# Sixteen single gate groups, the key norm ahead of the decay sums, and new order tables in a two-block transformer kernel

## What is computed

```python
proj = h @ w_in                                   # q, k, v of 8 heads, gate z (2048), 16 logits
qkv = silu(causal_depthwise_conv(qkv, conv_w))    # 4 taps
q, k = l2_norm(q) * 128 ** -0.5, l2_norm(k)
beta, g = sigmoid(b_logit), -exp(a_log) * softplus(a_logit + dt_bias)
# chunked, per head: g = cumsum(g); decay = exp(g_i - g_j) on the lower triangle
lower = strict_tril(beta * (k @ k.T) * decay)
u, w = solve(I + lower, [v * beta, k * beta * exp(g)])
qk = (q @ k.T) * decay
for each chunk:
    v_new = u_i - w_i @ S
    o = (q * exp(g))_i @ S + qk_i @ v_new
    S = S * exp(g_last) + (k * exp(g_last - g))_i.T @ v_new
o = rms_norm(o, o_gain) * silu(z)
x = x + o @ w_out
```

## Time and profile before

| | |
|---|---|
| median of 3 runs | 1658.16 us (1657.97 to 1661.1) |
| the profiled execution's own time | 1661.27 us |
| its span from first to last instruction | 1659.5 us |
| mean granted TensorE clock | 0.981 |
| head loop | about 65 to 530 us |

### The profile page before, as it was taken

One profiled execution on the slowest core, in us unless ns is written; L12 is line 12 of the kernel. 1 busy time (PEld: TensorE's weight loads), 2 busy tenths in 40 slices (PEclk: granted clock), 3 DMA queues, 4 the chain that ended last, 5 costly groups with the idle time before them and its releaser, 6 DMA issues.

```text
span 1659.5 us, 20679 instructions
## 1 busy us (share of the span) xinstructions
PE 1578.6 (95%) x7686; PEld 1240.5 (75%) x7686; DVE 875.4 (53%) x1633; ACT 746.9 (45%) x1293; POOL 244.3 (15%) x451
## 2 busy tenths in 40 slices
PE   6789999998989999999999899999999999999998
PEld 5577888887777876777777687666577888888876
DVE  4666667666663554555555533544347334343466
ACT  4443454345444244566556523555455433232343
POOL 1033224332331100223222300000000000000000
PEclk9799999999999999999999899999999999999999
DMA  4121112111112323222222122111132323232221
GB/s 178 64 77 39 64 51 77 52 52 39 51 38 73 126 89 107 76 81 67 77 69 73 52 96 90 64 52 51 39 102 66 112 89 102 92 106 94 93 86 64
DMA packets 40163, 127.22 MB, mean 77 GB/s; under 512 B 4576, under 2 KB 9104, under 8 KB 40064
## 3 DMA queue, kind: packets, MB, share of 16 engines
q1 hardware_dynamic: 38112, 121.65, 22.6%
q0 software_dynamic: 1040, 3.27, 0.6%
q10 hardware_dynamic: 912, 0.99, 0.2%
HBM read 122.69 MB, written 2.15 MB: 75 GB/s over the span
## 4 chain that ended last, share of the span: by engine, by line
PE 81%; DVE 7%; ACT 7%; issue 3%; POOL 1%; DMA 1%; SPq 0%; ACTq 0%; DVEq 0%; POOLq 0%
PE ps L776 79%; ACT L L1655 3%; DVE wl L1848 2%; DVE L L2331 1%; PE ps L1108 1%; PE ps L901 1%; ACT wh L1255 1%; DVE qkv L1884 1%; DMA wraw<-in_wa 1%; DVE qb L1933 1%; POOL L L2614 1%; ACT L L1607 0%; DVE h L2460 0%; DVE U L2184 0%; ACT xm L1790 0%
## 5 line engine op out<-in xcount | busy, mean ns | idle before, releaser
L776 PE MATMUL ps<-xr,wh 128*128 128x512 f32 x2752 | 906.2, 411 | 16.7 <-DVE wl L1848 15.3
L776 PEld LDWEIGHTS ps<-xr,wh 128*128 128x128 f32 x2752 | 506.9, 191 | 146.4 <-issue 40.5
L776 PE MATMUL ps<-xr,wl 128*128 128x512 f32 x1376 | 544.9, 396 | 0.0
L1848 DVE TENSOR_TENSOR wl<-wraw,wh 128x1024 fp32r<-128x1024 f32 x214 | 262.6, 1233 | 171.4 <-ACT wh L1255 169.7
L776 PEld LDWEIGHTS ps<-xr,wl 128*128 128x128 f32 x1376 | 262.1, 190 | 57.9
L1255 ACT ACTIVATE wh<-wraw 128x1024 fp32r<-128x1024 f32 x214 | 222.3, 1049 | 89.2 <-PE ps L776 85.3
L776 PE MATMUL ps<-xm,wh 128*128 128x512 f32 x640 | 200.0, 394 | 6.7 <-DVE xm L2445 3.7
L776 PEld LDWEIGHTS ps<-xm,wh 128*128 128x128 f32 x640 | 120.3, 189 | 35.3 <-DVE xm L2445 5.0
L2614 POOL TENSOR_SCALAR L<-L,m 128x256 f32<-128x256 f32 (+1 forms) x128 | 80.5, 649 | 317.0 <-DVE m L2346 317.0
L776 PE MATMUL ps<-xm,wl 128*128 128x512 f32 x320 | 125.3, 392 | 0.0
L1884 DVE SCALAR_TENSOR_TENSOR qkv<-cin,gains,qkv 128x512 f32<-128x512 f32 x96 | 73.7, 769 | 4.0 <-ACT qkv L1283 2.9
(11 more groups left out here) (258 smaller groups left out, 1793.3 us busy)
## 6 DMA issues: line engine op xcount, KB each, us to landing
wraw<-in_wa SPq DMA_DIRECT2D x48, 512.0 KB, 3.7
wraw<-in_wb SPq DMA_DIRECT2D x32, 512.0 KB, 3.9
wraw<-in_wu SPq DMA_DIRECT2D x32, 512.0 KB, 3.6
wraw<-in_wd SPq DMA_DIRECT2D x32, 512.0 KB, 3.7
wraw<-in_wao SPq DMA_DIRECT2D x16, 512.0 KB, 3.7
wraw<-in_wbo SPq DMA_DIRECT2D x16, 512.0 KB, 3.8
wraw<-in_wc SPq DMA_DIRECT2D x16, 512.0 KB, 3.7
bias<-rel_rows SPq DMA_DIRECT2D x16, 256.0 KB, 4.2
```

Of the source, the lines that this page charges most:

```text
L776: return e.matmul(out, w, x, start=start, stop=stop, skip_group_check=True)
L1848: e.tensor_tensor(m.wl[:, i % N_SPLIT, :], m.raw[:, i % N_RAW, :], m.wh[:, i % N_SPLIT, :].bitcast(F), ALU.subtract).then_inc(s.wlo, 1)
```

## The change

Three things change together. The z products, until now 8 pairs of groups, are 16 single groups: six in pass 1, one in each of passes 2 to 5, two in pass 6, one in pass 7, three in pass 8. In `prep` the sum of squares of k (`ks`) and its norm stand ahead of the decay's sums (`G`) and its exponential, and DVE's `dv` moves from its first piece to its fourth, right ahead of `y`; POOL's mask moves with it. And every order table (`PLAN`) is new, with `STEADY` replaced by the entry "a". The number of instructions and their sizes stay the same.

```diff
 PRODUCTS = {
-    1: (("head", 0), ("head", 1), ("z", 0), ("z", 1)),
-    2: (("head", 2), ("z", 2)),
-    3: (("head", 3), ("z", 3)),
-    4: (("head", 4), ("z", 4)),
-    5: (("head", 5), ("z", 5)),
-    6: (("head", 6),),
-    7: (("head", 7),),
-    8: (("z", 6), ("z", 7)),
+    1: (("head", 0), ("head", 1)) + tuple(("z", n) for n in range(6)),
+    2: (("head", 2), ("z", 6)),
+    3: (("head", 3), ("z", 7)),
+    4: (("head", 4), ("z", 8)),
+    5: (("head", 5), ("z", 9)),
+    6: (("head", 6), ("z", 10), ("z", 11)),
+    7: (("head", 7), ("z", 12)),
+    8: (("z", 13), ("z", 14), ("z", 15)),
 }
 def groups_of(what, h):
-    return [[("wa", 6 * h + j)] for j in (range(4) if what == "head" else range(4, 6))]
+    if what == "z":
+        return [[("wa", 6 * (h // 2) + 4 + h % 2)]]
+    return [[("wa", 6 * h + j)] for j in range(4)]
 PLAN = {
-    0: plan("g5 g4 g6"),
-    1: plan("p0 p5 p4 p0 p2 p2 p3 p2 p2 p4 p3 p2 p1 p2"),
-    2: plan("q1 q0 p0 p4 q0 p0 q2 p1 q1 p0 q0 p3 q0 p1 q2 p2 r1 r0 p0 r1 p1 r1 p2 r0 p1 r3 p2 r3 r0 p1 r0 r2 r2"),
-    HEADS: plan("q1 p0 q0 p3 q3 p0 q2 p0 q2 p0 q2 p3 q2 p0 q1 p1 r3 r1 r2 p1 p3 p0 r2 r1 p2 r3 p2 r0 r4 p5 r1 r5 r3"),
-    HEADS + 1: plan("q2 q4 q2 q3 q3 q2 q2 q0 r3 r1 r2 r3 r4 r0 r1 r1 r7 r4 r3"),
+    "a0": plan("g10 g9 g17"),
+    "a1": plan("p5 p8 p2 p1 p2 p3 p10 p6 p6 p9 p6 p11 p14 p8"),
+    "a2": plan("p2 p0 p0 q1 p2 q3 q1 p0 q5 q2 q0 p0 q2 p0 q3 r0 p1 r3 r1 r0 r1 p0 r1 r1 r4 p0 p1 r0 r2 p2 p5 p0 r1"),
+    "a8": plan("p0 q1 p2 q3 q1 q0 p0 q0 p3 q0 p0 q0 p0 q0 p1 r1 r0 r1 r0 p0 r0 p2 p0 r0 p0 r0 p2 r5 p0 r1 p0 r2 r1"),
+    "a9": plan("q1 q5 q2 q5 q3 q1 q3 q2 r9 r1 r3 r0 r1 r0 r2 r0 r4 r2 r4"),
+    "a": plan("p0 q2 q0 p4 q2 q0 p1 p1 q4 q0 p0 q1 p0 q1 p0 r2 r2 r0 p1 r0 p3 p1 r0 p2 r0 r1 r2 r3 p1 r2 p0 p2 r16"),
 }
-STEADY = plan("p1 q1 q2 p1 q2 p0 q0 q0 p0 p1 q0 p1 q1 p1 q2 r1 p3 r0 p3 r3 p2 r2 p0 r0 p4 r3 p1 r1 p3 r5 r3 r2 r1")
...
# PE, prep: the order of the first two products
-        e.wait_ge(s.gate_v, 12)
-        end(four(bank(), lambda n: m.gg[:, h, n:n + 1].to_broadcast([128, 128]), lambda n: m.triu),
-            (s.prep_v, prep_v(h, "dv")), (s.prep_a, prep_a(h, "eb")))
-        yield
-        yield
         cleared(PREP_BANK)
         e.wait_ge(s.prep_a, prep_a(h, "sqk"))
         end(mm(m.banks[PREP_BANK][:], m.ones, m.rq[:, 0, :]), (s.prep_a, prep_a(h, "lnk")))
+        yield
+        yield
+        if h == 0:
+            e.wait_ge(s.gate_v, 7)
+        end(four(bank(), lambda n: m.gg[:, h, n:n + 1].to_broadcast([128, 128]), lambda n: m.triu),
+            (s.prep_v, prep_v(h, "dv")), (s.prep_a, prep_a(h, "eb")))
...
# ACT, prep: the norm of k ahead of the exponential of G
-        e.wait_ge(s.prep_v, prep_v(h, "dv"))
-        if h:
-            e.wait_ge(s.prep_v, prep_v(h - 1, "qdn"))
-        did(e.activation(m.rq[:, 1, :], product("G"), ACT.Exp))
         did(e.activation(m.rq[:, 0, :], product("ks"), ACT.Ln, bias=m.const(C_EPS)))
         after("lnk")
         did(e.activation(m.rq[:, 0, :], m.rq[:, 0, :], ACT.Exp, scale=-0.5))
         yield
+        if h:
+            e.wait_ge(s.prep_v, prep_v(h - 1, "qdn"))
+        e.wait_ge(s.prep_v, prep_v(h, "dv"))
+        did(e.activation(m.rq[:, 1, :], product("G"), ACT.Exp))
+        yield
         e.wait_ge(s.prep_o, prep_o(h, "sel"))
         did(e.activation(m.Dm[:], m.Dm[:], ACT.Exp))
-        yield
...
# DVE, prep (POOL's mask moves by three pieces in the same way)
+        yield from idle(3)
         o = product("G")
         if h:
             e.wait_ge(s.prep_v, prep_v(h - 1, "qk"))
+        else:
+            e.wait_ge(s.gate_v, 10)
         did(e.tensor_tensor(m.Dm[:], o, bc(m.gsub[:, col]), ALU.subtract))
-        yield from idle(3)
         e.wait_ge(s.prep_a, prep_a(h, "exk"))
         did(e.tensor_tensor(k, k, m.rq[:, 0, :], ALU.mult))
```

More of the change, by code:

```diff
@@ L96 @@
 BLOCK = {kb: n for n, kb in enumerate(ORDER)}
-LATE_Z = tuple(h for i, p in PRODUCTS.items() for w, h in p if w == "z" and i >= min(h + 2, HEADS))
+LATE_Z = tuple(n // 2 for i, p in PRODUCTS.items() for w, n in p if w == "z" and n % 2 and i >= min(n // 2 + 2, HEADS))
 N_RAW, N_SPLIT, LEAD = 4, 4, 2
@@ L321, in follow @@
     banks(EARLY)
-    weave(g, PLAN[0], {"g": part("gates")}, p.get("tap"))
+    weave(g, PLAN["a0"], {"g": part("gates")}, p.get("tap"))
     out = gemm("ao", pair_groups("wao", 8), 3, None, 2)
@@ L336, in follow @@
             g = pieces_out("split_o", out, 3, 2, 0, 14)
-        weave(g, PLAN.get(i, STEADY), parts, p.get("tap"))
+        weave(g, PLAN.get(f"a{i}", PLAN["a"]), parts, p.get("tap"))
         drain(g)
@@ L683, in __init__ @@
         self.gs, self.gm, self.go = new("gate_sigmoid"), new("gate_times"), new("gate_out")
-PREP_P = {n: i + 1 for i, n in enumerate(("G", "ks", "kk", "qk", "kT", "v0", "v1"))}
+PREP_P = {n: i + 1 for i, n in enumerate(("ks", "G", "kk", "qk", "kT", "v0", "v1"))}
 PREP_A = {n: i + 1 for i, n in enumerate(
-    ("silu1", "sqk", "silu0", "silu2", "silu3", "eb", "lnk", "exk", "E", "sqq", "v0", "v1"))}
+    ("silu1", "sqk", "silu0", "silu2", "silu3", "lnk", "exk", "eb", "E", "sqq", "v0", "v1"))}
 PREP_V = {n: i + 1 for i, n in enumerate(("dv", "y", "at", "qk", "kg", "kd", "dc", "qdn", "U3", "T3"))}
@@ L755, in z_drain @@
 def z_drain(h, n):
-    return drained_before("z", h) + n + 1
+    return drained_before("z", 2 * h + n) + 1
 def head_drain(h, j):
@@ L815, in drained @@
         if name == "z":
-            return [(s.adrain, z_drain(a, n))]
+            return [(s.adrain, z_drain(a // 2, a % 2))]
         if name == "ao":
@@ L1902, in evac_z @@
         e.wait_ge(s.wused, i + 1)
-        e.tensor_tensor(m.XF[:, 16 + 2 * h + n, :], bank[:], m.rb_a[:], ALU.mult).then_inc(s.adrain, 1)
+        e.tensor_tensor(m.XF[:, 16 + h, :], bank[:], m.rb_a[:], ALU.mult).then_inc(s.adrain, 1)
     def evac_ao(n, bank, i, a):
@@ L2540, in prep @@
                             pattern=[[0, 4], [1, 128]], channel_multiplier=-1))
-        yield from idle(4)
+        yield
         if h == 0:
```

## The result

The changed kernel takes 1616.1 us (median of 4 runs, 1615.44 to 1616.42) against 1658.9 for the kernel before on the same chip (median of 4, 1657.97 to 1661.1). The ratio is 0.974 with a 95% interval of 0.9723 to 0.9756: faster by 42.8 us. The forecast was 1628, and the range 1617 to 1648 doesn't hold the measured time. Built and run once more on another chip, the same kernel took 1615.16 (ratio 0.9731, 0.9716 to 0.9745).

What follows compares the result with a forecast made beforehand. TensorE, busy 95%, bounds the kernel; waits and lower clock at both ends of the head loop are winnable. Gain 31.5 to `P4` of head 7 plus 2 in pass 9, less 3.5, is 30: 1658.2 - 30 = 1628 us, range 1617 to 1648.

Steps and rivals of the forecast that it cites:

- the price of the middle: Passes 2 to 7: a pass of 40 steps takes 48.7 us, pass 6 with 48 steps 54.1.
- the gain of 2 in pass 9: Pass 9: `s0` 9 steps behind `u0` removes a 2.01 us wait and slow stretch; `sum` waits 1 to 1.5.
- the 3.5: Deducted from the 33.5 us gain for what the walk misses: 0.4 in each of 9 passes.
- The tight places of the middle: Passes 2 to 7: `s0`/`s1`, `u1`, `ks` and `G` barely fit; 0.3 us a pass, 51 if each misses by 0.6.
- the 0.87 of `T5`: Old steady pass: `T5` right behind `U5` waits 0.87 us for DVE's update; the new table removes it.
- The start: Up to the first `P4`: third gates' product at 62.7, `ks` at 77.2, `P4` of head 0 at 118.5 us.
- Pass 8: 24 steps, 37.8 us of TensorE work; the inverse makes it 39.5, a wait of about 2 us.
- Half the gain: Rival: DVE late at `u1`, ScalarE at `ks`, 2.2 us in 7 passes: 1643; 0.27 together with the straight line.
- The inverse is late: Rival: taps and splits on DVE hold GpSimd, inverse outruns its 3.5 us margin; slower, 1670 if 6.5 late; chance 0.07.
- The estimate by proportion: Inverse on GpSimd: with DVE's share of a pass rising from 66% to about 70%, at most 1 us longer.
- Nothing, or the straight line: Rival: cover is only moved; no change (0.05), or 52.2 us per 40-step pass, 1647 (0.27 together with half the gain).
- More: Rival: no place waits and pass 8 neither; gain 38 to 40 us, 1619; chance 0.06.

Runs made afterwards that it cites:

- z-in-pairs run: The changed kernel with the z groups in pairs where they were, new order of `ks` and `G` and new tables kept: 1641.11 us, ratio 0.9879.

## Why the prediction was off in size

The direction, the places and the mechanism were right. What failed were sizes in the sum: the time was 12 us too long, because the gain was put too low at four places and 3.5 us were deducted on top, all on the same side. The three that weigh most are the price of the middle (48.7 a pass), the gain of 2 in pass 9, and the 3.5. In the profiled executions:

- **The tight places of the middle (0.3 a pass) and the 0.87 of `T5`.** The forecast was 54.71 - 5.44 - 0.87 + 0.3 = 48.7, with a lower bound of 48.4; measured are 47.7 to 48.1, below that bound. No tight place waits: from 117 to 446 us the profile lists 0.2 us of waits in all. And the new order is worth 1.58 in a 48-step pass, as the z-in-pairs run isolates, where the forecast had 0.87. The 0.7 between is in no list of waits, but the rows place it: from start to start the 48 product steps of such a pass take 35.6 us in the kernel before and 34.9 in that run. A step behind a small product takes 0.78 or more where the others take 0.68 to 0.70, and there are 18 of them before and 15 in that run. And the step ahead of `U4` takes 1.02 before, because `U4` stands one step behind `P4` and starts (232.12) only when ScalarE's copy is there (231.38 + 0.60); the new table has two steps between them. The two together make some 0.6 of the 0.7. Worth 3.8 us in passes 3 to 7 and 0.7 in pass 2.
- **The start.** Forecast at 118.5, measured 117.55, where the whole execution ran some 0.7 earlier from its first instructions (the gates' first product at 38.14, against 38.84). The step by step walk through DVE's and ScalarE's queue held to within 1 us at each of its points (62.7, 77.2 and 118.5 against 61.96, 76.61 and 117.55), and to 0.3 with those 0.7 taken off. One figure in it is wrong, without effect: had all 16 steps ahead of `ks` run at the lower clock, at twice 0.68, they would have ended near 85 and not at 77. Three of them did.
- **Pass 8.** A wait of 2 us for the inverse was forecast, 0.97 measured (38.61 against 39.5).
- **Pass 9 (2 us).** Measured 6.0. `s0` doesn't wait and neither does `sum`, whose 1 to 1.5 us the forecast charged. Its table alone is worth 3.1 to 3.9, by the run that takes it back; the remaining 2 to 3 us are busy time at the lower clock, which pass 9 had before and doesn't have with its old table in the new kernel. That this was inherited from a pass 8 with waits is argued: the run with pass 8's old table shows only 0.8 to 1.6 of it.
- **The 3.5 set against the sum.** Next to nothing answers to it (a late operand costs some 0.4 us in each of three passes of one profile of the kernel after, and nothing in the other: see the last section). A pass priced as the measured 54.71 less what is taken out of it already holds such small losses (this is argued). This was the one term without a row behind it, and it alone moved the forecast from 1624.5 to 1628.

Their sum is 3.8 + 0.7 + 1.0 + 0.9 + 4.0 + 3.5 = 13.9, on a gain of 30: 43.9. The rest of the kernel, from the first scaling on, took 1058.2 instead of 1059.6, with the same waits: 45.3, which is the 45.4 between the two profiled executions. The medians differ by less, 42.8, because the profiled one of before lay 2.4 above its median.

The rivals:

- **Half the gain** (`ks` and `u1` late in each pass) does not happen in this kernel, but the margin at `ks` is 0.23 us. With the old steady table it does happen at `ks`, and with the two other waits of a pass it costs more than four times the 2.2 a pass that the rival gave.
- **The inverse is late.** GpSimd's first product starts at 238.57 in a steady pass and the copy behind the last one at 252.99: 14.4, where before it was 15.0. `U3` and `T3` end 1.6 us before the next `P4`. Here are GpSimd's rows, and then DVE's beside them.

```profile
238.57 0.29 POOL L2589 TENSOR_TENSOR masks<-nb,uc 128x60 f32<-128x60 f32 x1 [8.76 <-DVE nb L2157]
...
247.02 1.32 POOL L2589 TENSOR_TENSOR masks<-nb,uc 128x24 f32<-128x24 f32 x1
...
252.99 2.55 POOL L2537 TENSOR_TENSOR Mm<-AT,masks 128x512 f32<-128x512 f32 x2
```

```profile
247.02 1.23 DVE L1852 TENSOR_TENSOR wl<-wraw,wh 128x1024 fp32r<-128x1024 f32 x1 [0.57 <-ACT wh L1259]
...
256.01 0.68 DVE L2167 TENSOR_TENSOR U<-uc,masks 128x512 f32<-128x512 f32 x1
256.72 0.71 DVE L2173 STREAM_TRANSPOSE Tm<-U 128x512 f32<-128x512 f32 x1
```

  Both engines' rows start at 247.02, and GpSimd's small product takes 1.32 where undisturbed ones of its size take 0.2 to 0.3. By the Trainium skill, SBUF — State Buffer, section "Who interferes with whom", the port pair that the two share is held for the whole instruction of the winner; this row agrees. But the chain as a whole is no longer for it, though DVE's share of the pass is larger, here 36.36 of 48.04 (76%) against 66% before. The estimate by proportion, up to 1 us longer, was too dark as well.
- **Nothing, or the straight line** (52.2 for 40 steps). Refuted for the whole change, and what happens when its first part stands alone. Under the old tables 40 steps take 49 to 53 and the gain is nil; the line was a good guess at a kernel whose tables stay.
- **More** (38 to 40, 1619) was the nearest. It got 0.06, on the ground that no place would wait. It should have been heavier: every bound on a tight place was taken on the side of a loss.

What held was the reading that the loss sat at both ends of the loop. With each moved product step counted at 0.68, the gain from the gates' first product to the first scaling divides like this:

| stretch | before | after | steps before, after | gain |
|---|---|---|---|---|
| start, to `P4` of head 1 | 136.75 | 125.17 | 144, 152 | 17.0 |
| passes 3 to 5 | 164.12 | 143.88 | 144, 120 | 3.9 |
| pass 6 | 48.80 | 53.51 | 32, 48 | 6.2 |
| pass 7 | 47.52 | 47.68 | 32, 40 | 5.3 |
| pass 8 | 48.92 | 38.61 | 32, 24 | 4.9 |
| pass 9 | 114.95 | 108.91 | none | 6.0 |

The sum is 43.3. The middle gives a tenth of it.

Open stays what the new tables are worth alone, without either of the other parts: that was not run.

## What to carry to other kernels

Where an order written by hand feeds an in-order TensorE, moving work to even out the passes is worth nothing until the order is made anew for the new counts: the spread of z gave nothing under the old tables, and 26 us under the new ones with `ks` first (1641.1 to 1615.2); with z spread and `G` first, the new tables gave 42 (1663.5 to 1621.5). A wait is worth removing only if it isn't the slack of another engine's chain; when one is shortened, look at which one grows, and put work there that needs nothing of the busy engines. In a forecast, don't deduct a lump for what might be missed when the price of a pass was read from a running one.

## What the runs showed that was not expected

- A wait costs more than its own length, and how much more depends on what follows. With the old steady table 6.3 us of waits in a pass cost 9.3 to 11 us: the granted clock of the pass was 0.90 to 0.95, partly at the lower of the two levels, 1.2 instead of 2.4 GHz.
- The same pass at the same table can differ in it. In pass 9 of the kernel after, TensorE idles 1.2 us from 446.99 to 484.25 and the clock is 0.95. In the second profile of the same kernel it idles 1.5 us in the same stretch and the clock is 1.00, from there to the first scaling too, and so it is with the old table, where it idles 4.9 us in 112.0. What sets when the clock falls is not settled by these runs.
- Which of two engines starts first, by 0.1 or 0.2 us, decides between two lengths of a pass. In passes 4 to 6 a tap on DVE and a mask product on GpSimd (`Mm`, line 2537) start at almost the same time. Whichever starts second takes longer than in the other order, the tap by 1.05 us and the product by 0.33: here is the pair of pass 5 in the kernel after, then the same pair in its second profile.

```profile
260.32 1.80 DVE L1888 SCALAR_TENSOR_TENSOR qkv<-cin,gains,qkv 128x512 f32<-128x512 f32 x1
260.21 1.36 POOL L2537 TENSOR_TENSOR Mm<-AT,masks 128x512 f32<-128x512 f32 x1 [4.67 <-PE ps L779]
```

```profile
260.21 0.75 DVE L1888 SCALAR_TENSOR_TENSOR qkv<-cin,gains,qkv 128x512 f32<-128x512 f32 x1
260.43 1.69 POOL L2537 TENSOR_TENSOR Mm<-AT,masks 128x512 f32<-128x512 f32 x1 [5.01 <-PE ps L779]
```

  A tap of 1.80 instead of 0.75 makes DVE's split and its transpose of `U` late, and `P5` starts 0.46 behind the last matmul ahead of it (264.79 to 265.25) instead of 0.24 (264.98 to 265.22) and takes 0.1 longer. The list of waits doesn't show it. In the seven profiles of kernels with these passes (the kernel after twice, and the runs with another table in the gates and pass 1, in pass 8 or in pass 9 or with z 0 and z 1 moved), the 12 passes in which GpSimd starts first take 48.04 to 48.13 us with 40 steps and 53.50 or 53.51 with 48, and the 9 in which DVE starts first take 47.69 to 47.79 and 53.15 to 53.17.
